# The second half of every streamed weight piece copied by ScalarE in place of GpSimd

## The reference

```python
def expert_block(args):
    xblk, e = args
    g = xblk @ w_gate[e] + b_gate[e]
    u = xblk @ w_up[e] + b_up[e]
    g = jnp.minimum(g, SWIGLU_LIMIT)
    u = jnp.clip(u, -SWIGLU_LIMIT, SWIGLU_LIMIT)
    act = (u + 1) * g * jax.nn.sigmoid(SWIGLU_ALPHA * g)
    return act @ w_down[e] + b_down[e]
```

## Time and profile before

| | |
|---|---|
| median of 3 runs | 1646.23 us (1645.62 to 1653.6) |
| profiled execution | 1658.77 us, span from first to last instruction 1655.9 us |
| PE busy | 1434.4 us, 87% of the span |
| POOL busy | 899.9 us, 54% |
| DVE busy | 494.1 us, 30% |
| ACT busy | 241.9 us, 15% |
| mean clock granted to PE | 0.942 of full |
| moved by DMA | 533.83 MB, 322 GB/s over the span |

### The profile page before, as it was taken

How to read it: one execution, slowest core, us unless ns; L and a number is a source line. 1 busy time by engine, 2 the same in 40 slices (tenths; PEclk the granted TensorE clock), 3 DMA queues, 4 the chain that set the end, 5 groups by cost and what they waited for, 6 DMA issues and landing times.

```text
span 1655.9 us, 54045 instructions
## 1 busy us (share of the span) xinstructions
PE 1434.4 (87%) x21389; PEld 828.1 (50%) x21389; DVE 494.1 (30%) x970; ACT 241.9 (15%) x654; POOL 899.9 (54%) x864
## 2 busy tenths in 40 slices
PE   6998999886888988988998888988889889988886
PEld 3885576564444444444444444444445444544443
DVE  2224445335222223222232222322223222322223
ACT  2113433211100001101011000110001000010001
POOL 0000000010667777777776777777777777777773
PEclk9998999887898899999999999999999989999897
DMA  8956489600899999999999999899998999989992
GB/s 337 371 207 223 151 312 350 234 25 11 316 360 360 374 369 356 357 376 375 360 357 373 372 370 366 344 368 375 374 376 339 376 370 363 381 343 374 373 369 112
DMA packets 153031, 533.83 MB, mean 322 GB/s; under 512 B 9677, under 2 KB 26693, under 8 KB 149918
## 3 DMA queue, kind: packets, MB, share of 16 engines
q1 hardware_dynamic: 151694, 528.75, 82.9%
q0 software_dynamic: 1296, 4.49, 0.7%
HBM read 530.23 MB, written 2.97 MB: 322 GB/s over the span
## 4 chain that ended last, share of the span: by engine, by line
POOL 32%; PE 28%; DMA 24%; issue 7%; POOLq 3%; DVE 3%; SPq 2%; ACT 1%; DVEq 0%; ACTq 0%
POOL mem L472 32%; PE ps L499 25%; DMA arena<-in_w_gate 15%; DMA arena<-in_w_down 3%; DMA arena<-in_cache_k 2%; DMA arena<-in_w_up 2%; POOLq L472 2%; PE ps L673 1%; DMA mem<-in_w_in 1%; SPq L372 1%; POOLq L469 1%; POOLq L470 1%; DVE arena L970 1%; PE ps L958 0%; PE ps L648 0%
## 5 line engine op out<-in xcount | busy, mean ns | idle before, releaser
L472 POOL COPY mem<-arena 128x1024 f32 x840 | 889.0, 1058 | 400.2 <-POOL mem L472 195.3
L499 PE MATMUL ps<-arena,hT 128*32 128x256 f32 (+1 forms) x7840 | 524.3, 403 | 144.9 <-DMA arena<-in_w_gate 109.5
L499 PE MATMUL ps<-mem,hT 128*32 128x256 f32 (+2 forms) x7584 | 478.8, 381 | 2.9 <-DMA mem<-in_w_in 2.9
L499 PEld LDWEIGHTS ps<-arena,hT 128*32 128x32 f32 (+1 forms) x7840 | 248.3, 123 | 395.9 <-DMA arena<-in_w_gate 162.4
L499 PEld LDWEIGHTS ps<-mem,hT 128*32 128x32 f32 (+1 forms) x7584 | 289.9, 118 | 179.4 <-issue 31.9
L499 PE MATMUL ps<-arena 128*32 128x259 f32 (+5 forms) x4376 | 220.3, 360 | 17.8 <-ACT arena L1492 3.2
L1340 DVE TENSOR_SCALAR hT<-ps 128x256 f32<-128x256 f32 x70 | 29.7, 425 | 664.9 <-PE ps L499 664.9
L499 PEld LDWEIGHTS ps<-arena 128*32 128x32 f32 (+3 forms) x4376 | 121.4, 112 | 102.3 <-issue 55.0
L457 POOL DMA_DIRECT2D arena<-in_b_gate x2 | 1.0, 492 | 188.6 <-DVE arena L1185 188.6
L970 DVE TENSOR_TENSOR arena<-arena,ps 128x1152 f32<-128x1152 f32 (+1 forms) x71 | 94.2, 1326 | 11.8 <-PE ps L499 11.5
L1349 DVE TENSOR_SCALAR mem<-ps 128x256 f32<-128x256 f32 x70 | 29.7, 424 | 217.0 <-PE ps L499 217.0
(11 more groups left out here) (193 smaller groups left out, 662.1 us busy)
## 6 DMA issues: line engine op xcount, KB each, us to landing
arena<-in_w_gate SPq DMA_DIRECT2D x140, 1024.0 KB, 8.1
arena<-in_w_up SPq DMA_DIRECT2D x140, 1024.0 KB, 7.3
arena<-in_w_down SPq DMA_DIRECT2D x140, 1024.0 KB, 7.0
mem<-in_w_ada SPq DMA_DIRECT2D x24, 1024.0 KB, 8.2
arena<-in_cache_k SPq DMA_DIRECT2D x56, 384.0 KB, 6.8
arena<-in_cache_v SPq DMA_DIRECT2D x56, 384.0 KB, 4.9
mem<-in_w_in SPq DMA_DIRECT2D x12, 1024.0 KB, 11.9
mem<-in_w_out SPq DMA_DIRECT2D x4, 1024.0 KB, 9.1
```

The source lines that it names most:

```text
L472: pool.tensor_copy(mem[:, ds(light * (SLOTS * PIECE - home) + home, SPILL)], stage[:, j % STAGES, h * SPILL:(h + 1) * SPILL]).then_inc(hel ...
L499: return te.matmul(out, a, b, start=first, stop=last)
```

## The change

What POOL did alone is divided: POOL copies the first half of each piece (columns 0 to 1023 of the slot), ACT the second half, each at its own pace, with a semaphore each (`held_in[0]`, `held_in[1]`). POOL issues 12 copies a turn in place of 24; ACT gets 12 copies of 128x1024 f32 from SBUF to SBUF that it did not have. ACT is the engine that serves the chain of activations, so the program places its copies: those of the 4 gate pieces in front of the sigmoids, those of the 4 up pieces behind them, those of the 4 down pieces behind `copy_x` and in front of the two `ye` copies. SyncE and PE wait for both semaphores; PE waits for the second one only in the middle of each piece. The activation buffers `tu` and `sg` are moved to other places in SBUF, since there are two spill places now. `wait_passed` becomes the same semaphore as `pe_passed`; it only counts that waits were passed.

```diff
--- before.py
+++ after.py
@@ -81,7 +81,7 @@
 PAIR = 2
 NB = PAIR * TURNS
 TABS = 3 * 2 * HD + 384 + KEYS + NSEQ * NSAMP + 2 * PAIRS * NSAMP
-SPILL = PIECE // 2
+HALF = PIECE // 2
 MOVED = -10000.0
 
 
@@ -179,6 +179,7 @@
         tail_col = view(o, 8); o += 8
         exp_row = view(o, TURNS); o += TURNS
         light_row = view(o, TURNS); o += TURNS
+        sg0 = view(o, 256); o += 256
         assert o <= o_s - XTRA, (o, o_s)
         c_part, c_cnt, c_more, c_one, c_off, c_heavy, c_light, c_first, c_end, c_free, c_rows = (
             col[:, i:i + 1] for i in range(11))
@@ -224,8 +225,9 @@
         qTs = mem[:, o:o + PAIRS * NSAMP].rearrange("p (h n) -> p h n", n=NSAMP); o += PAIRS * NSAMP
         kTs = mem[:, o:o + PAIRS * NSAMP].rearrange("p (h n) -> p h n", n=NSAMP); o += PAIRS * NSAMP
         assert o == SLOTS * PIECE + TABS
-        free = [mem[:, o - 256 * (i + 1):o - 256 * i] for i in range((TABS - SPILL) // 256)]
-        tu, sg = free[0:2], free[2:4]
+        tu = [mem[:, o - 256:o], flat_h[:, 256 * 8:256 * 9]]
+        sg = [sg0, sb("sg1", [P, 256])[:, :]]
+        assert 2 * HALF + 256 <= TABS
         cst = sb("cst", [P, 2 * NSEQ * KC])
         stat = sb("stat", [P, 16])
         eps = sb("eps", [P, 1])
@@ -299,7 +301,8 @@
         y_sq, y_std = sem("y_sq"), sem("y_std")
         moe_zeros, own_spread = sem("moe_zeros"), sem("own_spread")
         stage_in = [sem(f"stage_in{j}") for j in range(STAGES)]
-        held_in, wait_passed = sem("held_in"), sem("wait_passed")
+        held_in = [sem(f"held_in{i}") for i in range(2)]
+        wait_passed = pe_passed
 
         counts = {}
 
@@ -419,8 +422,9 @@
                     if not isinstance(t, int) or EXP_PIECES * t + j >= STAGES:
                         sp.wait_ge(piece_used[0], EXP_PIECES * t + (j - STAGES + 1))
                         sp.sem_inc(wait_passed, 1)
-                        sp.wait_ge(held_in, 2 * EXP_PIECES * t + 2 * (j - STAGES + 1))
-                        sp.sem_inc(wait_passed, 1)
+                        for h in range(2):
+                            sp.wait_ge(held_in[h], EXP_PIECES * t + (j - STAGES + 1))
+                            sp.sem_inc(wait_passed, 1)
                     r = (j % 4) * 256
                     src = (w_gate, w_up, w_down)[j // 4][0, ds(e, 1), r:r + 256, :]
                     sp.dma_start(stage[:, j % STAGES, :].rearrange("p (k c) -> p k c", c=D),
@@ -456,21 +460,30 @@
                              (brrow[0:1, :], b_router), (iota, c_iota), (tri, c_tri)):
                 pool.dma_start(dst, src).then_inc(in_moe, 16)
 
+            def where_to(t):
+
+                at = light_row[0:1, t:t + 1] if isinstance(t, int) else light_row[0:1, ds(t, 1)]
+                return pool.value_load(at.bitcast(I32), min_val=0, max_val=1)
+
+            def hold(light, t, j):
+
+                pool.wait_ge(stage_in[j % STAGES], 48 * t + 16 * (j // STAGES + 1))
+                pool.sem_inc(wait_passed, 1)
+                if not isinstance(t, int) or t > 0:
+                    pool.wait_ge(piece_used[1], EXP_PIECES * t + (j - EXP_PIECES + 1))
+                    pool.sem_inc(wait_passed, 1)
+                if not isinstance(t, int) or t > 0 or j > 0:
+                    pool.wait_ge(held_in[0], EXP_PIECES * t + j)
+                    pool.sem_inc(wait_passed, 1)
+                home, spill = j * PIECE + 0 * HALF, SLOTS * PIECE + 0 * HALF
+                pool.tensor_copy(mem[:, ds(light * (spill - home) + home, HALF)],
+                    stage[:, j % STAGES, 0 * HALF:1 * HALF]).then_inc(held_in[0], 1)
+
             def turn(t):
 
-                at = light_row[0:1, t:t + 1] if isinstance(t, int) else light_row[0:1, ds(t, 1)]
-                light = pool.value_load(at.bitcast(I32), min_val=0, max_val=1)
+                light = where_to(t)
                 for j in range(EXP_PIECES):
-                    pool.wait_ge(stage_in[j % STAGES], 48 * t + 16 * (j // STAGES + 1))
-                    if not isinstance(t, int) or t > 0:
-                        pool.wait_ge(piece_used[1], EXP_PIECES * t + (j - EXP_PIECES + 1))
-                    for h in range(2):
-                        if not isinstance(t, int) or t > 0 or j > 0 or h > 0:
-                            pool.wait_ge(held_in, 2 * EXP_PIECES * t + (2 * j + h))
-                        pool.sem_inc(wait_passed, 1)
-                        home = j * PIECE + h * SPILL
-                        pool.tensor_copy(mem[:, ds(light * (SLOTS * PIECE - home) + home, SPILL)],
-                                         stage[:, j % STAGES, h * SPILL:(h + 1) * SPILL]).then_inc(held_in, 1)
+                    hold(light, t, j)
 
             pool.wait_ge(blk_ready, 2)
             turn(0)
@@ -866,10 +879,11 @@
                     te.wait_ge(stage_in[j % STAGES], 48 * b + 16 * (j // STAGES + 1))
                     W = stage[:, j % STAGES, :].rearrange("p (k c) -> p k c", c=D)
                 else:
-                    te.wait_ge(held_in, 2 * EXP_PIECES * b + 2 * (j + 1))
                     W = slot_w(j, rows=True)
                 q1 = j % 4
                 for c in range(2):
+                    if i == 1:
+                        te.wait_ge(held_in[c], EXP_PIECES * b + (j + 1))
                     for q in range(4):
                         last = mm(ps[32 * q:32 * q + 32, bank + i, 0:256], x[i][:, c * P + 32 * q1:c * P + 32 * q1 + 32],
                                   W[:, c, q * 256:(q + 1) * 256], j == DOWN[0] and c == 0, j % 4 == 3 and c == 1)
@@ -1552,6 +1566,25 @@
             se.wait_ge(gsT_made, 1)
             copy(gsT[0:NEXP, :], ps[0:NEXP, 4, 0:NT], gsT_ready)
 
+            def where_to(t):
+
+                at = light_row[0:1, t:t + 1] if isinstance(t, int) else light_row[0:1, ds(t, 1)]
+                return se.value_load(at.bitcast(I32), min_val=0, max_val=1)
+
+            def hold(light, t, j):
+
+                se.wait_ge(stage_in[j % STAGES], 48 * t + 16 * (j // STAGES + 1))
+                se.sem_inc(wait_passed, 1)
+                if not isinstance(t, int) or t > 0:
+                    se.wait_ge(piece_used[1], EXP_PIECES * t + (j - EXP_PIECES + 1))
+                    se.sem_inc(wait_passed, 1)
+                if not isinstance(t, int) or t > 0 or j > 0:
+                    se.wait_ge(held_in[1], EXP_PIECES * t + j)
+                    se.sem_inc(wait_passed, 1)
+                home, spill = j * PIECE + 1 * HALF, SLOTS * PIECE + 1 * HALF
+                se.copy(mem[:, ds(light * (spill - home) + home, HALF)],
+                    stage[:, j % STAGES, 1 * HALF:2 * HALF]).then_inc(held_in[1], 1)
+
             def copy_rows(b):
                 for i in range(PAIR):
                     se.wait_ge(x_made, 2 * b + (i + 1))
@@ -1566,11 +1599,16 @@
 
             def turn(b, first=False, last=False):
 
+                light = where_to(b)
+                for j in GATE:
+                    hold(light, b, j)
                 for i in range(PAIR):
                     se.wait_ge(g_clipped, 2 * b + (i + 1))
                     if not first:
                         se.wait_ge(act_ready, 2 * b + (i - 1))
                     se.activation(sg[i], tg[i], ACT.Sigmoid, scale=ALPHA).then_inc(g_sig, 1)
+                for j in UP:
+                    hold(light, b, j)
                 if not last:
                     copy_rows(b + 1)
                 for i in range(PAIR):
@@ -1578,12 +1616,15 @@
                     se.copy(actT[i], ps[:, 4 + i, 0:256]).then_inc(actT_ready, 1)
                 if not last:
                     copy_x(b + 1)
+                for j in DOWN:
+                    hold(light, b, j)
                 for i in range(PAIR):
                     se.wait_ge(piece_used[i], EXP_PIECES * (b + 1))
                     se.copy(ye[i], ps[:, 4 + i, 0:256]).then_inc(ye_ready, 1)
 
             copy_rows(0)
             copy_x(0)
+            se.wait_ge(blk_ready, 2)
             turn(0, first=True)
             with se.Fori(1, TURNS - 1) as b:
                 turn(b)
```

## The result

The changed kernel took 1689.38 us (median of 4 runs, 1688.68 to 1696.27), the kernel before 1646.24 us (median of 4). The ratio is 1.026 (95% interval 1.022 to 1.030): 43 us slower, where the prediction had 1649 us and a range to 1670.

The account below looks back on a forecast made before the run. Bound by DMA pieces every 2.56 us plus a 3.5 us hole between turns, not POOL. ACT free, start, copy and SyncE gave +0.09 us a turn, +3 us over 34 turns: 1649 us on the 1646.23 median, range 1637 to 1670.

Parts of the forecast that it names:

- What bounds the kernel: One turn's path: twelve pieces landing every 2.56 us, then a 3.5 us hole; POOL is not on it.
- the hole between the turns: Turn's end: 3.5 us in which the down pieces have landed and PE can't yet use the first.
- The relief on VectorE: Before the down stage: VectorE's table pair no longer held up by POOL's copies, ACT through 0.48 us earlier, PE 0.46.
- The four terms of the new issue time: Next turn's first gate issue: ACT free 969.45, start 0.10, copy 1.05, SyncE 0.23; 970.83 against 970.74.
- SyncE's long wait: Sign in the profile after: SyncE's longest wait, 6.2 us for PE before, would be for ACT's copy.
- The step that failed: Gate issues after a turn's first: 1.3 us apart in place of some 0.9, hidden since pieces land every 2.56 us.
- Pieces 2.56 us apart: Sign in the profile after: pieces of the stream still land every 2.56 us.
- The rivals: Alternatives to no change: slower (0.37), faster through PE's earlier down stage (0.12), faster through the stream (0.03).
- The one on the slower side: No relief on VectorE, 1666 us, or ACT's copy starting late, 1669 us; chance 0.37.
- Its worst price of 1691 us: Slower case with every bound bad but the copy's: next gate issue at 972.06, +1.3 us a turn.
- TensorE's clock: Sign of being wrong: PE at its lower clock more often; mean 0.942 before, a drop in the up stage on the path.

## Why the prediction was wrong, point by point

**What bounds the kernel** was right: the path by pieces, PE and the hole between the turns. The experiments moved the mean turn, between 33.96 and 35.61 us, by what they did to that path, and the times followed where they are settled.

**The relief on VectorE** came as computed. PE's down stage starts 1.03 us behind its transposes in place of 1.49, the value that the first turn gave. The Trainium skill (SBUF — State Buffer, Who interferes with whom) has the port pair between VectorE and GpSimd as an exclusive lock that ScalarE has no part in; the runs agree, with the 0.51 us mean of VectorE's table line with the copies on ScalarE and 0.70 us with the down copies back on GpSimd.

**The four terms of the new issue time** held. ScalarE's copy starts at 630.37, as L1598 ends at 630.38, where I took 0.10; it takes 1.05; the issue follows its end (631.41) by 0.28, where I took 0.23. The issue comes 3.00 us behind the start of the transposes, where the sum had 3.07. One sign was named wrongly: SyncE's long wait was to be for ScalarE's copy, but it stayed the one for TensorE, with 7.3 us. What sets the issue is the short wait behind it.

**The step that failed** is this one: "The next three gate pieces are issued 1.3 us apart in place of some 0.9 [...], still faster than 2.56, hidden too." The spacing was right, 1.22 us. The conclusion wasn't: that an issue costs nothing as long as it is ahead of the stream. Issued 1.22 us behind the first, which came behind a hole in the stream, the second piece lands 1.24 us later on average than when it is issued 0.91 us behind. That is +1.24 us a turn, set at 0; "Pieces 2.56 us apart", one of the signs named, is what failed. With it the sum is 1649 + 34 x 1.24 = 1691 us, against 1689. The match is closer than the working: by the growth of the whole turn in the two traces, 1.10 us, it would be 1646 + 34 x 1.10 = 1684 us.

**The rivals** missed it too. The one on the slower side had the relief lost or ScalarE late; neither happened. Its worst price of 1691 us was near the result by chance. The turns of before couldn't show what a wider spacing does, because SyncE's spacing there was 0.91 to 0.92 us in each; a bound from both sides was due on this term as on the others, and the range was too narrow without it.

**TensorE's clock** was not the cause. The mean granted was 0.927 in place of 0.942, but the stretches in which PE sets the end took 11.47 and 11.49 us.

## What to carry to other kernels

The first transfer behind a hole in the stream was a special place here: the one that follows it did best issued at once (0.91 us or less), and better clearly later (1.7 us) than in between. So the landing of the second one has to be looked at whenever the spacing of the issues changes. A change of 0.16 us on an issuing engine cost 19 to 31 us here, by one run, and a delay put in on purpose gave 30 us back. When work goes to an engine that also serves a chain, place each piece by when its data has landed and the engine is free (the first two down copies), not by stage.

## What wasn't expected of the hardware

Two DMAs of 1 MB on one queue, the first behind a hole in the stream: with 0.91 us or less between the issues the second landed 2.6 to 2.7 us behind the first, with 0.97 us 2.8, with 1.07 to 1.31 us 3.5 to 3.9 us behind it, with 1.7 us and more again 2.9 to 3.0. The first bytes of the first one moved 1.0 us behind its issue, about where the bad band begins; that the two are connected was not tried.

The last down piece need not have landed for it. In eight of the 33 turns of the changed kernel the first gate piece was issued up to 1.54 us before it had; in seven of these the second piece came as late as elsewhere, 3.76 to 4.09 us behind the first, and in one (0.42 us before) it came 2.57 us behind it, at the same spacing of 1.22 us. Little was moving by then, though: behind the issue at 1307.19, with the landing 1.54 us off, some 27 GB/s. Whether nearly idle DMA engines are needed was not tried. Why the second piece is served late, and why that one turn was spared, stays open.
